# Seven of nine projection tiles of the first key head inside the last recurrence, in a buffer shared with the recurrence's logarithms

## The reference, cut to what matters

```
h = RMSNorm(x) * (1 + scale1) + shift1
q, k, v, rq, rf_fwd, rf_bwd, ri, rg, za, zr = split(h @ w_in)
rec  = RMSNorm(HGRN2_fwd + HGRN2_bwd) * silu(rg)      # 8 heads, chunks of 64 tokens
q, k = rope(RMSNorm(q)), rope(RMSNorm(k))             # 16 heads, 4 key heads
x = x + gate1 * (sigmoid(za) * attention(q, k, v) + sigmoid(zr) * rec) @ w_o
x = x + gate2 * ConvFFN(RMSNorm(x) * (1 + scale2) + shift2)
```

## Time and profile before

| | us |
|---|---|
| median of 3 runs (2793.96 to 2795.63) | 2794.38 |
| the profiled execution | 2795.13 |
| its span, first to last instruction | 2793.3 |
| TensorE busy | 2659.3 (95%) |
| VectorE, ScalarE, GpSimd busy | 1632.2, 1026.2, 808.1 |
| TensorE idle between recurrent and attention stage | 13.5 |

### The profile page before, as it was taken

How to read it: one execution, slowest core, us unless ns; L and a number is a source line. 1 busy time by engine, 2 the same in 40 slices (tenths; PEclk the granted TensorE clock), 3 DMA queues, 4 the chain that set the end, 5 groups by cost and what they waited for, 6 DMA issues and landing times. The chain is left out here.

```text
span 2793.3 us, 41424 instructions
## 1 busy us (share of the span) xinstructions
PE 2659.3 (95%) x15169; PEld 2438.1 (87%) x15169; DVE 1632.2 (58%) x2601; ACT 1026.2 (37%) x1899; POOL 808.1 (29%) x775
## 2 busy tenths in 40 slices
PE   5899999999999799999999989799999999999998
PEld 2799999999999687768878867599999999999997
DVE  3245255255255447776777675625677766677765
ACT  3223233233233226666566666623222122221214
POOL 0222122122122143252352231742322222222222
PEclk9899999999999899999999999899999999999999
DMA  9311111111011110010020010231111111111101
GB/s 372 117 38 44 30 42 42 29 43 42 29 43 35 45 34 9 1 60 1 8 68 8 1 51 1 84 112 31 53 45 38 45 38 45 38 45 38 45 23 75
DMA packets 164252, 135.99 MB, mean 49 GB/s; under 512 B 18461, under 2 KB 141885, under 8 KB 164157
## 3 DMA queue, kind: packets, MB, share of 16 engines
q1 hardware_dynamic: 162940, 130.02, 14.8%
q10 hardware_dynamic: 1216, 4.72, 0.4%
HBM read 120.44 MB, written 14.29 MB: 48 GB/s over the span
## 5 line engine op out<-in xcount | busy, mean ns | idle before, releaser
L335 PE MATMUL proj_ps<-act_hi,w_hi 128*128 128x384 f32 x1152 | 410.4, 356 | 4.3 <-POOLq L472 4.3
L335 PE MATMUL ffn_ps<-act_hi,w_hi 128*128 128x384 f32 (+2 forms) x1128 | 384.3, 341 | 12.9 <-PEq L974 8.1
L336 PE MATMUL proj_ps<-act_lo,w_hi 128*128 128x384 f32 x1152 | 390.6, 339 | 0.0
L337 PE MATMUL proj_ps<-act_hi,w_lo 128*128 128x384 f32 x1152 | 390.4, 339 | 0.0
L337 PE MATMUL ffn_ps<-act_hi,w_lo 128*128 128x384 f32 (+2 forms) x1128 | 383.5, 340 | 0.0
L336 PE MATMUL ffn_ps<-act_lo,w_hi 128*128 128x384 f32 (+2 forms) x1128 | 383.4, 340 | 0.0
L2392 DVE SCALAR_TENSOR_TENSOR resid_t<-ffn_ps,mod,resid_t 128x384 f32<-128x384 f32 (+2 forms) x640 | 273.9, 509 | 139.3 <-PE ffn_ps L337 139.3
L1745 DVE TENSOR_TENSOR probs_lo<-att_ps,probs_hi 128x512 fp32r<-128x512 f32 x324 | 223.1, 689 | 157.4 <-ACT att_ps L1542 153.6
L1541 ACT ACTIVATE probs_hi<-att_ps 128x512 fp32r<-128x512 f32 x324 | 193.9, 598 | 198.7 <-PE att_ps L1361 197.8
L2370 DVE SCALAR_TENSOR_TENSOR conv<-up,conv_t,conv 128x127 f32<-128x127 f32 (+1 forms) x168 | 212.0, 1321 | 77.8 <-ACT conv L2298 66.0
L482 POOL CAST w_hi<-w_raw 128x1024 fp32r<-128x1024 f32 x48 | 61.8, 1287 | 636.6 <-PE proj_ps L337 601.8
(11 more groups left out here) (285 smaller groups left out, 5839.3 us busy)
## 6 DMA issues: line engine op xcount, KB each, us to landing
w_raw<-in_w_in SPq DMA_DIRECT2D x64, 512.0 KB, 3.9
ada_w<-in_ada_w SPq DMA_DIRECT2D x12, 2048.0 KB, 14.7
w_raw<-in_w_up SPq DMA_DIRECT2D x44, 512.0 KB, 3.9
w_raw<-in_w_down SPq DMA_DIRECT2D x22, 512.0 KB, 3.6
rec_scratch<-rec_out SPq DMA_DIRECT2D x8, 576.0 KB, 2.8
out<-xy SPq DMA_DIRECT2D x9, 512.0 KB, 2.6
w_raw<-in_w_o SPq DMA_DIRECT2D x8, 512.0 KB, 5.4
xy<-in_x_sample SPq DMA_DIRECT2D x8, 512.0 KB, 5.9
```

Of the source, the lines that this page charges most:

```text
L335: nc.tensor.matmul(out, w_hi, x_hi, start=(k == 0), stop=False)
L336: nc.tensor.matmul(out, w_hi, x_lo, start=False, stop=False)
L337: return nc.tensor.matmul(out, w_lo, x_hi, start=False, stop=last)
```

## The change

`QKV`, until now allocated in `phase2`, is allocated before `phase1` and given to both. GB and BB become views of it; together they have exactly its size (3 x 1152 = 9 x 384 columns). Seven of the nine tiles move into the last recurrence, in thirds: two thirds among the transposes (after tiles 7 and 8), four among the chunk states (after tiles 1, 3, 5, 7), one ahead of each sum of squares, the other twelve at the end. ScalarE evacuates tile 0 before the gate ZR, tile 1 after it, tiles 2 to 6 after the roots. It also waits for VectorE's last reading of the logarithms before its first copy. `phase2` keeps tiles 7 and 8; its counts of `proj_done` and `proj_out` are lowered by seven, and ScalarE's order there is changed. The orders of SyncE and GpSimd are as before.

```diff
+NT_EARLY = 7
+            QKV = sb("qkv", [P, NT, G], c=mid)
@@ phase1
-        GB = sb("log_f", [P, 2, T])
-        BB = sb("cum_log_f", [P, T])
+        logs = QKV[:, :, :].rearrange("p t c -> p (t c)")
+        GB, BB = logs[:, 0:2 * T].rearrange("p (d t) -> p d t", d=2), logs[:, 2 * T:3 * T]
...
+                thirds = [(t, part) for t in range(NQ) for part in range(3)]
+                def qkv_third():
+                    t, part = thirds.pop(0)
+                    k0, k1 = THIRDS[part]
+                    if part == 0:
+                        if t == 0:
+                            pe.wait_ge(w_split, RH * NU + 3 + C_SPLIT)
+                        pe.wait_ge(proj_out, RH * PG + t - 1 + C_OUT)
+                    cols = slice(t * P, (t + 1) * P)
+                    for k in range(k0, k1):
+                        nc.tensor.matmul(proj[:, t % 2, 0:G], HH[:, k, cols], WH[:, :, k, :], start=(k == 0), stop=False)
+                        nc.tensor.matmul(proj[:, t % 2, 0:G], HL[:, k, cols], WH[:, :, k, :], start=False, stop=False)
+                        m = nc.tensor.matmul(proj[:, t % 2, 0:G], HH[:, k, cols], WL[:, :, k, :], start=False, stop=(k == KC - 1))
+                    if k1 == KC:
+                        m.then_inc(proj_done, 1)
                 r = RH - 1
                 for j in range(NT):
                     transposes(r, j)
+                    if j >= 7:
+                        qkv_third()
                 for j in range(NT):
                     chunk_states(r, j)
+                    if j % 2:
+                        qkv_third()
...
                 for g in range(NG):
+                    qkv_third()
                     sum_squares(r, g)
+                while thirds:
+                    qkv_third()
@@ phase1, scalar
+                def qkv_out(t):
+                    act.wait_ge(proj_done, RH * PG + t + 1 + C_PROJ)
+                    nc.scalar.activation(QKV[:, t, :], proj[:, t % 2, 0:G], ACT.Copy).then_inc(proj_out, 1)
                 r = RH - 1
+                act.wait_ge(dir_ready, r * 2 + 3)
                 for j in range(0, NT, 2):
                     keys_values(r, j)
+                qkv_out(0)
                 zr_gate(r)
+                qkv_out(1)
...
                 for g in range(NG):
                     norm_root(r, g)
+                for t in range(2, NQ):
+                    qkv_out(t)
@@ phase2
-                for t in range(NT):
+                for t in range(NT_EARLY, NT):
                     projected(t)
@@ phase2, scalar
                 act.wait_ge(set_ok, 3)
-                for t in range(3):
-                    projected_out(t)
                 nc.scalar.preload_act_table_set(LN_EXP)
                 squares(0)
-                projected_out(3)
+                projected_out(7)
                 norm_ln(0, 15)
                 norm_exp(0, 15)
-                for t in (4, 5):
-                    projected_out(t)
+                projected_out(8)
                 squares(1)
-                projected_out(6)
                 norm_ln(0, 15)
                 norm_exp(0, 15)
-                for t in (7, 8):
-                    projected_out(t)
+                first_gate_out(0)
                 squares(2)
                 norm_ln(0, 15)
                 norm_exp(0, 15)
-                for n in range(3):
+                for n in range(1, 3):
                     first_gate_out(n)
```

More of the change, by code:

```diff
@@ L102, in build @@
         phase0(nc, a, sb, pb, sem, W, w_in, (B_RQ, B_RFF, B_RFB), HH, HL, ident, ones, CW, MOD, A1, A2, lb, lb1, lb1n, rgain)
-        spent = sems[:]
-        phase1(nc, a, sem, W, w_in64, HH, HL, ident, ones, lb, lb1, lb1n, rgain, w_in, rec_dram, out_state, spent)
-        for done in spent:
-            nc.release_semaphore(done)
-        phase2(nc, a, sem, W, w_o, HH, HL, ident, w_in, w_in64, rec_dram, mix_dram, out_k, out_v)
+        with ExitStack() as mid:
+            QKV = sb("qkv", [P, NT, G], c=mid)
+            spent = sems[:]
+            phase1(nc, a, sem, W, w_in64, HH, HL, ident, ones, lb, lb1, lb1n, rgain, w_in, rec_dram, out_state, spent, QKV)
+            for done in spent:
+                nc.release_semaphore(done)
+            phase2(nc, a, sem, W, w_o, HH, HL, ident, w_in, w_in64, rec_dram, mix_dram, out_k, out_v, QKV)
         X1 = sb("resid_t", [P, KC, T])
@@ L402, in phase1 @@
         C_SPLIT, C_PROJ, C_OUT = 2, 9, 2
+        NQ = NT_EARLY
         FWD = [(c, 18 if c == 1 else c + 1) for c in range(NCH)]
@@ L754, in gates @@
                         ch.link(nc.vector.tensor_copy(EL[:, d, :], last))
-                        ch.link(nc.vector.tensor_tensor(KD[:, d, :], SIG[:, d, :], BB[:, :], ALU.mult))
+                        ch.link(nc.vector.tensor_tensor(KD[:, d, :], SIG[:, d, :], BB, ALU.mult))
                         nc.vector.tensor_tensor(SIG[:, d, :].rearrange("p (c t) -> p c t", t=CH), KD[:, d, :].rearrange("p (c t) -> p c t", t=CH),
@@ L1072, in split @@
                     if m == 1 or m == 2 or m == 3:
-                        pool.wait_ge(proj_done, NT)
+                        pool.wait_ge(proj_done, NT - NT_EARLY)
                     elif m == 4:
-                        pool.wait_ge(proj_done, NT + 6)
+                        pool.wait_ge(proj_done, NT - NT_EARLY + 6)
                     elif kind == "o":
@@ L1366, in weighted @@
                         if s < 2:
-                            pe.wait_ge(proj_out, NT + 6)
+                            pe.wait_ge(proj_out, NT - NT_EARLY + 6)
                         else:
@@ L1485, in projected_out @@
                 def projected_out(t):
-                    act.wait_ge(proj_done, t + 1)
+                    act.wait_ge(proj_done, t - NT_EARLY + 1)
                     nc.scalar.activation(QKV[:, t, :], ps[:, B_PROJ + t % 2, 0:G], ACT.Copy).then_inc(proj_out, 1)
                 def squares(g):
-                    act.wait_ge(proj_out, 3 * g + 3)
+                    if 3 * g + 3 > NT_EARLY:
+                        act.wait_ge(proj_out, 3 * g + 3 - NT_EARLY)
                     if g:
@@ L1554, in gate_sigmoid @@
                 def gate_sigmoid(kv):
[L1555 removed]
+                    act.wait_ge(f_out if kv else proj_out, F_AT["g", kv, 5] + 1 if kv else NT - NT_EARLY + 6)
                     nc.scalar.activation(ZA[:, :, :], ZA[:, :, :], ACT.Sigmoid).then_inc(za_sig, 1)
                 act.wait_ge(set_ok, 3)
[L1559 to L1560 removed]
                 nc.scalar.preload_act_table_set(LN_EXP)
                 squares(0)
[L1563 removed]
+                projected_out(7)
                 norm_ln(0, 15)
                 norm_exp(0, 15)
[L1566 to L1567 removed]
+                projected_out(8)
                 squares(1)
[L1569 removed]
                 norm_ln(0, 15)
                 norm_exp(0, 15)
[L1572 to L1573 removed]
+                first_gate_out(0)
                 squares(2)
```

18 lines of the change are left out of this document (7 added, 11 removed).

## The result

| | before | after |
|---|---|---|
| median (lowest to highest), 6 runs each | 2794.39 (2793.96 to 2795.63) | 2805.45 (2802.61 to 2806.56) |
| ratio, 95% interval | | 1.0038 (1.0028 to 1.0048) |
| profiled execution | 2795.13 | 2806.56 |
| its span | 2793.3 | 2804.8 |
| TensorE busy | 2659.3 | 2666.8 |

What follows compares the result with a forecast made beforehand. TensorE, busy 95%, was taken as the bound, but after the change late loads and the serial norm chain: 11.75 + (51.9 - 56.6) + 2.4 = +9.5 us, giving 2804 us, range 2795.5 to 2808.

Steps and rivals of the forecast that it cites:

- rival A: Attention stage: late weight landing, GpSimd's first split, then serial norm chain set the path; 2799 to 2808 us, chance 0.78.
- B: Attention stage's start: weights land 7.8 us after it, late landing being only the moment's; +1.5 us, 2796, chance 0.10.
- C: Attention stage to second key transposes: TensorE's own work decides, transposes 20 us early; 2774 us, chance 0.06.
- D: Last recurrence: moved thirds hurt it more, all 5.2 us unhidden and 2 more in the tail; 2810 us, chance 0.06.
- Step 1: Last recurrence's transposes: TensorE waits 1.2 us for the third weight split, two thirds go in; chunk states +3.6 us.
- Step 2: Chunk states: four thirds (5.2 us) mostly hidden, cost +1.4 us; sums of squares begin 5.0 us later, at 942.84.
- Step 3: Recurrence's tail: TensorE ends last, then evacuation and barrier 1.2 us; P, the attention stage's start, +11.75 us at 966.7.
- Step 4: After the attention stage's start: weights cast 15.8 us later, split done at 19.3; TensorE waits 11 us, first Newton step queues.
- The rule against the row: Gain broadcasts: skill page's rule gives 16 DMA engines, the trace's 0.07 share looked like about one in sixteen.
- Step 5: Norm chain: three serial groups, 32.0 us, then the keys' low part; second key transposes at 1018.7, +7.1 us.
- Step 6: Second key transposes: TensorE restarts at half clock after about 5 us idle; +2.4 us, bounds 0 and 2.5.
- The sum: At the second key transposes: 11.75 + (51.9 - 56.6) + 2.4 = +9.5 us, which nothing later takes in.

Runs made afterwards that it cites:

- e3: Changed kernel with only the two gate units' raw weights loaded early, gains left in the stage's list: 2798.79 us, ratio 1.0015.
- e8: Changed kernel with the two weight loads ahead of the gains in the attention stage's list: 2803.34 us, ratio 1.0032.
- e9: Changed kernel with each gain broadcast replaced by a same-size copy from 128 different rows: 2797.15 us, ratio 1.0009.
- e2: Kernel before, with gains and first two gate units' raw weights loaded early, in the recurrent stage: 2793.11 us, ratio 0.9997.
- e5: Changed kernel with three tiles moved instead of seven, all behind the sums of squares, gains and raw gate weights loaded early: 2780.46 us, ratio 0.9949.
- e6: Changed kernel with three tiles moved instead of seven, all behind the sums of squares, load list as it was: 2790.62 us, ratio 0.9989.
- e7: Kernel before with only the shared buffer and ScalarE's added wait, no tile moved: 2793.80 us, ratio 0.9997.
- e1: Changed kernel with gains and first two gate units' raw weights loaded early, in the recurrent stage: 2792.37 us, ratio 0.9991.
- e4: Changed kernel with all 21 thirds behind the last sum of squares, none inside the recurrence: 2807.03 us, ratio 1.0052.
- e11: Changed kernel measured once more, no edit: 2804.40 us, ratio 1.0038.

## Why the prediction was right, step by step

The forecast, 2804.0 within 2795.5 to 2808.0, stands against 2805.45 and 2804.40. The path was the one of rival A, step by step; none of B, C and D came. The sizes:

| step | predicted | measured, in before's frame |
|---|---|---|
| 1, chunk states begin | 915.55 | 915.74 |
| 2, first sum of squares begins | 942.84 | 945.71 |
| 3, P | 966.7 | 967.85 |
| 4, cast of the first gate's weights | P+15.8 | P+15.2 |
| 4, TensorE's wait for the split | 11 | 10.1 |
| 5, norm chain | 32.0 | 31.9 |
| 5, second key transposes | 1018.7 | 1018.99 |
| 6, clock | +2.4 | +3.3 |

**Step 1** was right in its mechanism: TensorE waits 1.06 us for the third split (1.2 predicted), then two thirds. (By the prediction's own terms it should read 913.61 and 915.50; 0.05 was added without a word.)

**Step 2** is the term that was mis-sized. The first scores of the second tile came at 928.44 in before's frame, against 922.19 before: 6.25 us later, not 5.0. The rows show what was left out: between the last projection matmul and the first chunk state lie 916.79-916.52=0.27 us, where two projection matmuls are 0.17 apart. At the other end of a third it is the same, so each third between the chunk states lasted 0.21 us more than its matmuls (17.88 to 19.13 is 1.25 for six, where 6 x 0.173 is 1.04). Over the six thirds, the two of step 1 with 0.11 and 0.18, this adds up to 1.1 of the 1.25 us; that is a sum over rows and assumes that none of it is hidden, and no run isolates it. The sums of squares were 2.9 us later than I said; the first sum now has a third ahead of it (1.6 us), which I had counted under step 3 and named under step 2, and the rest is this.

**Step 3** came out 1.15 us late, at +12.9: TensorE's end 1.6 late, mostly by what steps 1 and 2 were short, evacuation and barrier 0.4 early. TensorE was the late one, as predicted: VectorE's last product ends at 958.46 in before's frame, its store is issued within 0.1 us, and P is 9.4 us later. The evacuation of the seventh tile with the barrier was 0.76 us (968.14 to 968.90) behind TensorE's last matmul, where I had put 1.2.

**Step 4** was right in time and incomplete in its reason. I named the weights' landing and GpSimd's order, and not VectorE's own wait for the gains, which are in the same list. It had no part in the result, since the weights land behind the gains. But it is why e3 and e8 give less than the weights' landing alone would make one expect. It also belongs to the condition of rival B: with the weights early and the gains late (e8) the time is 2803, not B's 2796. With both early B's price holds: e9 has the landing that B supposed (cast at P+7.9), the split done at P+11.3, the transposes at P+43.8 where B said 43.9, and 2797.15 us.

**The rule against the row** was a misreading. The prediction took the DMA share of 0.07 for one engine in sixteen and set it against a rule that gives sixteen. A mean share doesn't say how many engines worked, and that rule says nothing of how fast a copy is, so it didn't foretell rival B. The packets show copies cut into the same pieces and slow in their pace (e9). The forecast did not rest on it: it took the landing, P+15.8, from the earlier trace rows.

**Step 5** was right within 0.1 us: 7.39+2.91+9.63+2.95+8.98=31.9 us, where the prediction had taken each link from the trace of the kernel before. A serial chain with no wait for TensorE in it can be carried over as it stands. TensorE's two further gaps of 6.0 and 5.3 us were foretold as 7 and 5.

**Step 6** was in the right direction, and 0.9 low; the bound of 2.5 that I set was too low. The windows of the changed kernel, where TensorE begins again after 5.3 us of idle:

```profile
1015.00:1020.00 5.00, 0.00 (x0) 0.00 (x0) 3.02 (x4) 0.00 (x0) 4.92 (x8) 0.75 0.00 0
1020.00:1025.00 5.00, 4.96 (x15) 3.30 (x16) 0.55 (x1) 0.49 (x1) 4.84 (x6) 0.50 0.00 1
1025.00:1027.00 2.00, 2.00 (x8) 1.82 (x7) 0.00 (x0) 0.00 (x0) 2.00 (x1) 0.50 0.85 251
```

The clock is at 1.2 GHz (0.50) for at least 7 us from 1020, where it was 5 in the earlier trace rows. It had been back at 2.4 GHz (1.00) in the window from 1015 to 1017 and fell while TensorE stood. The stretch from the second key transposes to the context step measures it in each kernel: 21.7 us before and in e2, e5, e6 and e7, where TensorE had stood for 0 to 2.4 us; 23.6 to 25.0 in the changed kernel, e1, e3, e4 and e8 to e11, where it had stood for 3.6 to 5.3. So the price of this restart was 2.0 to 3.3 us in eight traces, and 0 where TensorE hardly waited.

**The sum** was +9.5; it was 7.45+3.3=10.75. The 1.25 us between them are +1.15 (steps 1 to 3), -0.8 (P to the transposes, 51.1 instead of 51.9: the landing 0.6, the rest in small pieces) and +0.9 (clock). They partly cancel, and that much is luck. In the profiled execution the 1.05 of offset come on top, and 0.3 go after the context step: 11.5. The offset belongs to that execution; the changed kernel's runs lie up to 4 us apart, and their medians are 1.5 and 0.4 above the forecast.

**The rivals.** C (2774) needed chain and landing under 36.8 us together. Even e1 did not come there: from P to the second key transposes it took 1006.38-967.27=39.1 us, with TensorE still waiting 4.9 of them for the keys. D (2810) had P 5.8 us later than the forecast, at 972.5; it was 967.85.

## What to carry to other kernels

Before work is moved out of a stage, look at what runs beneath it: a serial chain of other engines and a queue of loads that were covered become the path as soon as the cover is shorter than they are. Move only as much as the idle time holds (three tiles, not seven), and in the same edit start earlier what stood under the cover; e5 had both and was the only kernel that gained more than 0.2%, while either half of it alone (e2, e6) gave 0.1% or less. Where several loads feed one chain, all of them must come early: bringing forward one hands most of the wait to the next (of the 12.1 us that e1 takes off the Newton step, e3 takes 4.4 and e8 1.2).

## What the runs showed of the hardware

- A copy of one 256-byte row to 128 partitions is slow, and holds what is queued behind it: the median of four was 7.4 us to landing and that of the weights behind them 11.9, against 2.4 and 4.7 where the source rows differ; the DMA share was 0.07 meanwhile. SyncE's issue of the cached keys, which stand behind both, took 8.31 us instead of 1.01; where they follow the gains without the weight loads between (e3, e8) it took 0.43.
- A stretch of projection matmuls among the chunk states costs 0.1 us at each end: 0.27 to 0.29 us to the next start instead of 0.17.
- The stretch at half clock after idle time differs from place to place and from run to run: TensorE was at half clock for about 5 us in the earlier trace rows and for at least 7 from 1020 in the changed kernel, and at the start of the recurrent stage until 100 in one execution and past 102 in another. What decides it stays open.
